# A two-block transformer kernel: who loads the constants, how piece 0 is rounded, and who closes the last norm

## The reference

```python
h = rmsnorm(x, attn_norm[layer])
x = x + even_mixer(h, even_w_in[e], ...)          # layer 0: h @ w_in comes first
...
f = (jax.nn.gelu(gate, approximate=True) * val) @ w_down[l]
h = h + rms_norm(f, ln_ffn_post[l])               # the end: x * rsqrt(mean(x*x) + eps) * gain, plus h
return h
```

## Time and profile before

| | us |
|---|---|
| median of 3 runs (lowest, highest) | 1922.12 (1921.83, 1923.32) |
| the profiled execution | 1921.35 |
| its span, first to last instruction | 1919.6 |
| TensorE busy | 1888.2 (98%) |
| VectorE busy | 997.7 (52%) |
| ScalarE busy | 740.3 (39%) |
| GpSimd busy | 179.4 (9%) |

### The profile page before, as it was taken

How to read it: one execution, slowest core, us unless ns; L and a number is a source line. 1 busy time by engine, 2 the same in 40 slices (tenths; PEclk the granted TensorE clock), 3 DMA queues, 4 the chain that set the end, 5 groups by cost and what they waited for, 6 DMA issues and landing times.

```text
span 1919.6 us, 26779 instructions
## 1 busy us (share of the span) xinstructions
PE 1888.2 (98%) x10729; PEld 1527.4 (80%) x10729; DVE 997.7 (52%) x1418; ACT 740.3 (39%) x1111; POOL 179.4 (9%) x215
## 2 busy tenths in 40 slices
PE   9999999999999999999999999999999999999998
PEld 7875788888888777788888888777879778888887
DVE  5456443434335686553343434759563576656523
ACT  4247432222234575542222323554342454333322
POOL 2001210000001100010000000303551100000001
PEclk9999999999999999999999999999999999999999
DMA  6310132232322202123223232321120223232321
GB/s 209 97 45 1 50 108 90 87 109 87 110 87 80 72 23 67 45 91 107 90 87 109 88 110 88 101 88 44 24 68 25 88 79 108 87 108 88 109 88 66
DMA packets 137795, 158.74 MB, mean 83 GB/s; under 512 B 15976, under 2 KB 125552, under 8 KB 137712
## 3 DMA queue, kind: packets, MB, share of 16 engines
q1 hardware_dynamic: 136272, 155.01, 24.9%
q0 software_dynamic: 1440, 2.58, 0.4%
HBM read 153.89 MB, written 3.68 MB: 82 GB/s over the span
## 4 chain that ended last, share of the span: by engine, by line
PE 91%; DVE 6%; ACT 2%; issue 1%; POOL 0%; ACTq 0%; DVEq 0%
PE bank L2894 35%; PE bank L2927 17%; PE bank L2426 14%; PE bank L2451 3%; PE bank L2981 2%; PE bank L2570 2%; PE bank L2945 2%; PE bank L2840 1%; PE bank L2873 1%; PE bank L2598 1%; PE bank L2689 1%; PE bank L2585 1%; PE bank L2512 1%; PE bank L2542 1%; DVE XL L1590 1%
## 5 line engine op out<-in xcount | busy, mean ns | idle before, releaser
L2894 PE MATMUL bank<-XH,w_hi 128*128 128x512 f32 x992 | 386.8, 390 | 0.7 <-DVE arena L1890 0.7
L2894 PE MATMUL bank<-XH,w_lo 128*128 128x512 f32 x992 | 385.9, 389 | 0.0
L2894 PE MATMUL bank<-XL,w_hi 128*128 128x512 f32 x992 | 385.9, 389 | 0.0
L2894 PEld LDWEIGHTS bank<-XH,w_hi 128*128 128x128 f32 x992 | 186.2, 188 | 40.0 <-DVE arena L1890 0.9
L2894 PEld LDWEIGHTS bank<-XL,w_hi 128*128 128x128 f32 x992 | 186.2, 188 | 38.9 <-issue 0.5
L2894 PEld LDWEIGHTS bank<-XH,w_lo 128*128 128x128 f32 x992 | 186.2, 188 | 38.8
L2426 PE MATMUL bank<-XH,w_hi 128*128 128x512 f32 x448 | 178.9, 399 | 2.6 <-DVE w_lo L1583 2.4
L2426 PE MATMUL bank<-XL,w_hi 128*128 128x512 f32 x448 | 175.2, 391 | 0.0
L2426 PE MATMUL bank<-XH,w_lo 128*128 128x512 f32 x448 | 175.0, 391 | 0.0
L1583 DVE TENSOR_TENSOR w_lo<-w_raw,w_hi 128x2048 fp32r<-128x2048 f32 (+5 forms) x67 | 116.4, 1757 | 94.0 <-ACT w_hi L1037 93.6
L1937 DVE TENSOR_TENSOR w_lo<-w_raw,w_hi 128x2048 fp32r<-128x2048 f32 x24 | 55.0, 2292 | 173.2 <-ACT w_hi L1348 173.2
(11 more groups left out here) (459 smaller groups left out, 3333.6 us busy)
## 6 DMA issues: line engine op xcount, KB each, us to landing
w_raw<-in_ffn_w_gate SPq DMA_DIRECT2D x22, 1024.0 KB, 5.1
w_raw<-in_ffn_w_up SPq DMA_DIRECT2D x22, 1024.0 KB, 5.1
w_raw<-in_ffn_w_down SPq DMA_DIRECT2D x22, 1024.0 KB, 4.8
w_raw<-in_w_up SPq DMA_DIRECT2D x22, 1024.0 KB, 4.9
w_raw<-in_w_in SPq DMA_DIRECT2D x13, 1024.0 KB, 5.1
w_raw<-in_w_down SPq DMA_DIRECT2D x11, 1024.0 KB, 4.9
w_raw<-in_even_w_in SPq DMA_DIRECT2D x8, 1024.0 KB, 5.0
w_raw<-in_even_w_out SPq DMA_DIRECT2D x4, 1024.0 KB, 5.0
```

The source lines that it names most:

```text
L2894: m = pe.matmul(bank[b][:, :], w[:, k, P * c:P * (c + 1)], x[:, k, :], start=(k == 0 and j == 0), stop=(k == KT - 1 and j == 2))
```

## The change

- The loads of the constants and of the vectors are issued by ScalarE's queue, as its first two instructions, and no more by SyncE.
- The warm-up of TensorE has four matmuls, not five.
- `XH` of piece 0 is made from bank 4 directly. ScalarE waits for the vectors and the transposed piece; VectorE's copy of piece 0 from the bank to `X` now waits for this rounding (`norm_hi`), and `low` of piece 0 waits for the copy's own increment.
- At the end VectorE multiplies the second half of each row block by the gain row as soon as the sums are there (`gained`), and, when the reciprocal root has come, scales that product and adds the residual in one operation (`closed`). The first halves of blocks 0 to 2 go as before (scaling by VectorE, add by GpSimd). In the last block both halves go the new way, and the first half is multiplied before the second half's square is there. SyncE's waits follow.

```diff
--- before.py
+++ after.py
@@ -768,9 +768,6 @@
 
         @block.sync
         def _(sp):
-            sp.dma_start(con[:, 0:2 * P], d["const_cols"][:, 0:2 * P]).then_inc(setup_loaded, 16)
-            sp.dma_start(vrow[:, :, :], d["vec_rows"].rearrange("(a p) n -> p a n", p=P)).then_inc(setup_loaded, 16)
-
             def load(slot, src):
                 kt, n = src.shape[1], src.shape[2]
                 dst = w_raw[:, slot, 0:kt * n].rearrange("p (t n) -> p t n", n=n)
@@ -857,10 +854,10 @@
             for t in range(ST):
                 rows = slice(P * t, P * (t + 1))
                 for n in range(2):
-                    if t == ST - 1 and n == 1:
-                        sp.wait_ge(normed_out, KT + 1)
+                    if t == ST - 1 or n == 1:
+                        sp.wait_ge(normed_out, KT + t + 1 + (t == ST - 1 and n == 1))
                     else:
-                        sp.wait_ge(out_added, 2 * t + n + 1)
+                        sp.wait_ge(out_added, t + 1)
                     cols = slice(512 * n, 512 * (n + 1))
                     sp.dma_start(out[0][rows, cols], fin[:, t, cols]).then_inc(stored, 16)
             sp.wait_ge(stored, 16 * 2 * ST)
@@ -924,11 +921,10 @@
                     gains = d["vec_rows"][at:at + KT, :].rearrange("a p -> (a p)").unsqueeze(0)
                     pool.wait_ge(normed_out, KT)
                     pool.dma_start(gain_row, gains.broadcast_to([P, D])).then_inc(side_loaded, 16)
-                    for t in range(ST):
-                        for n in range(2 if t < ST - 1 else 1):
-                            o = feature_blocks(fin[:, t, 512 * n:512 * (n + 1)])
-                            pool.wait_ge(scaled_out, KT + 2 * t + n + 1)
-                            pool.tensor_tensor(o, o, token_major(n, t), ALU.add).then_inc(out_added, 1)
+                    for t in range(ST - 1):
+                        o = feature_blocks(fin[:, t, 0:512])
+                        pool.wait_ge(scaled_out, KT + 2 * t + 2)
+                        pool.tensor_tensor(o, o, token_major(0, t), ALU.add).then_inc(out_added, 1)
                 if s == "mla":
                     sum_squares("mla")
                     sum_squares("q")
@@ -1017,6 +1013,9 @@
         def _(act):
             links = [0]
 
+            act.dma_start(con[:, 0:2 * P], d["const_cols"][:, 0:2 * P]).then_inc(setup_loaded, 16)
+            act.dma_start(vrow[:, :, :], d["vec_rows"].rearrange("(a p) n -> p a n", p=P)).then_inc(setup_loaded, 16)
+
             def link(ins):
                 links[0] += 1
                 ins.then_inc(act_link, 1)
@@ -1240,7 +1239,9 @@
                     high(name, k)
 
             def even():
-                high("even", 0)
+                act.wait_ge(turned_out, 1)
+                act.wait_ge(turned, 2)
+                act.activation(XH[:, 0, :], bank[4][:, :], ACT.Copy, scale=gain_of("even", 0)).then_inc(norm_hi, 1)
                 act.wait_ge(w_first, 16)
                 act.activation(w_hi[:, 0, 0:1024], w_raw[:, 0, 0:1024], ACT.Copy).then_inc(w_hi_ready, 1)
                 for k in range(1, 4):
@@ -1730,8 +1731,11 @@
             def even():
                 for f in range(KT):
                     dve.wait_ge(turned, f + 2)
+                    if f == 0:
+                        dve.wait_ge(norm_hi, split_base["even"] + 1)
                     dve.tensor_copy(X[:, f, :], bank[4 + f % 4][:, :]).then_inc(turned_out, 1)
                     if f == 0:
+                        dve.wait_ge(turned_out, 2)
                         low("even", 0)
                     if f == 1:
                         dve.wait_ge(w_hi_ready, 1)
@@ -1992,19 +1996,34 @@
 
             def last_norm():
 
+                def gained(t, n):
+                    cols = slice(512 * n, 512 * (n + 1))
+                    dve.tensor_tensor(fin[:, t, cols], bank[2 * t + n][:, :], gain_row[:, cols], ALU.mult)\
+                       .then_inc(scaled_out, 1)
+
+                def closed(t, n):
+                    o = feature_blocks(fin[:, t, 512 * n:512 * (n + 1)])
+                    dve.scalar_tensor_tensor(o, o, frstd[:, t:t + 1], token_major(n, t), ALU.mult, ALU.add)\
+                       .then_inc(normed_out, 1)
+
+                last = ST - 1
                 dve.wait_ge(side_loaded, 64)
                 for t in range(ST):
+                    if t == last:
+                        dve.wait_ge(sq_ready, n_sq + 2 * t + 1)
+                        gained(t, 0)
                     dve.wait_ge(sq_ready, n_sq + 2 * t + 2)
                     dve.scalar_tensor_tensor(fmean[:, t:t + 1], fsq[:, 2 * t:2 * t + 1], EPS, fsq[:, 2 * t + 1:2 * t + 2],
                                              ALU.add, ALU.add).then_inc(out_mean, 1)
+                    gained(t, 1)
                     dve.wait_ge(rstd_ready, len(NORMS) + t + 1)
-                    for n in range(2):
-                        cols = slice(512 * n, 512 * (n + 1))
-                        dve.scalar_tensor_tensor(fin[:, t, cols], bank[2 * t + n][:, :], frstd[:, t:t + 1],
-                                                 gain_row[:, cols], ALU.mult, ALU.mult).then_inc(scaled_out, 1)
-                o = feature_blocks(fin[:, ST - 1, 512:D])
-                dve.wait_ge(scaled_out, KT + 2 * ST)
-                dve.tensor_tensor(o, o, token_major(1, ST - 1), ALU.add).then_inc(normed_out, 1)
+                    if t < last:
+                        dve.scalar_tensor_tensor(fin[:, t, 0:512], bank[2 * t][:, :], frstd[:, t:t + 1],
+                                                 gain_row[:, 0:512], ALU.mult, ALU.mult).then_inc(scaled_out, 1)
+                    dve.wait_ge(scaled_out, KT + 2 * t + 1 + (t == last))
+                    if t == last:
+                        closed(t, 0)
+                    closed(t, 1)
 
             def taps(i, c, half, t):
 
@@ -3320,7 +3339,7 @@
                     rows(k, stop=(k == 3))
 
             pe.wait_ge(setup_ready, 1)
-            for j in range(5):
+            for j in range(4):
                 pe.matmul(bank[2][:, 0:2 * P], sq_acc[:, 0:P], sq_acc[:, 0:2 * P], start=True, stop=True)
             pe.wait_ge(setup_loaded, 32)
             for j in range(3):
```

## The result

| | before | changed |
|---|---|---|
| median, 22 executions each | 1922.02 | 1925.24 |
| lowest, highest | 1919.79, 1923.47 | 1922.65, 1927.76 |
| the profiled execution | 1921.35 | 1922.65 |
| its span | 1919.6 | 1920.8 |

The changed kernel is slower: ratio 1.0018, 95% interval 1.0012 to 1.0024, about 3.2 us. The forecast was 1921.6, in a range from 1920.0 to 1923.4: the measured median lies above it. The loss is just under the 0.2% that the prediction named as measurable; with 22 executions of each the interval excludes no change.

The account below looks back on a forecast made before the run. TensorE, busy 98% of the span, was taken as the bound, leaving the first 13 and last 6 us. Opening -0.7 and end +0.2 took 1922.12 to 1921.6 us, range 1920.0 to 1923.4.

Parts of the forecast that it names:

- Opening, the queue: Opening: constants issued by ScalarE let SyncE's loads be issued 0.9 us earlier; piece 4's landing taken as 0.7 us earlier.
- The DMA gate: Opening: piece 4's landing, which holds TensorE until about 12.9 us; said to move -0.7, bounds 0 and -0.9.
- the first rival: Opening: landings don't move, piece 4 stays at 12.3, the opening gives 0, total 1922.3; chance 0.2.
- rival 5: Opening: constants on ScalarE's queue land later; landing at 5.7 would cost 0.5 of the 0.7, total 1922.1; chance 0.05.
- Opening, the chain: Opening: shorter warm-up and direct rounding move VectorE's series about -0.7 us; first product near 9.0 instead of 9.85.
- rival 4: Opening: shorter warm-up leaves TensorE at its lower clock longer; opening +0.6, first product at 10.2, total 1922.9; chance 0.08.
- End: Last row blocks: the new split, with GpSimd's additions holding VectorE's means, costs +0.2 us, bounds -1.1 and +1.1.
- Rivals 2 and 3: End: GpSimd's additions come ahead of closings, +1.1, 1922.5; or the exclusion doesn't hold, -1.1, 1920.3; chance 0.12 each.
- the bound without exclusion: End: VectorE and GpSimd don't hold each other up, last closing at 1915.97, so -1.1 us.
- the rule was read from other rows: End: a VectorE operation with two SBUF inputs and a GpSimd addition exclude each other; whoever comes second waits.

Follow-up runs that it names:

- warm_only: Kernel before with four warm-up matmuls instead of five; median 1922.33, ratio 1.0004 (0.9995 to 1.0013).
- rest_only: Changed kernel with the two loads of constants and vectors back on SyncE's queue; median 1921.83, ratio 0.9998 to the kernel before.
- end_vector: Kernel before with the new end made on VectorE alone, no additions by GpSimd; median 1920.53, ratio 0.9999 (0.9990 to 1.0008).
- end_only: Kernel before with only the new closing of the last norm; median 1921.53, ratio 0.9999 (0.9990 to 1.0008).

## Why the prediction was wrong

- **Opening, the queue: the step that failed.** "The DMA gate, bounds 0 and -0.9; I take -0.7." In the trace it was +0.1: piece 4 landed at 12.4, where I had 11.6 and where it was 12.3 before. The slow stretch of the earlier trace rows was read as a hole that earlier work fills; it moved along. This step accounts for 0.7 of the 3.6 us between forecast and result. This is the first rival, which had 0.2, and the rule of the Trainium skill in "DMA: Bandwidth & Descriptors", "Issuing engines are not separate DMA queues", that only issue time is saved: the trace agrees for the weights and piece 4, issued 0.9 and 1.4 us earlier and landed 0.1 later. Piece 0 did land 2.0 us earlier, at the vectors' cost, which landed 1.6 later.
- **The missing bound: the step that cost most.** Worse than the size was the sign. I bounded the edit at 0 on the side of loss, and priced constants that come late (rival 5) at 0.5 of the gain with a chance of 0.05. Moved alone the constants cost 3.2 and 3.1 us. The rows on record showed enough to be wary: 320 KB that had a start of 0.9 us over SyncE's other loads were to lose it.
- **Opening, the chain: right in order, short in size.** First product at 9.40 (said 9.0), XL of piece 1 over at 12.56 (said 12.2). The vectors' transposes began at 5.41 by their landing, not by the warm-up, which cost 0.2 us. The first product then stood behind the transposes of piece 1, which waited 0.87 us for that piece and began at 8.79, and XL of piece 0 was over only at 9.26; the prediction had no term for the landing of piece 1. One matmul of warm-up less and the direct rounding alone gave nothing that can be measured, as a gate on DMA at 12.3 to 12.4 says they must.
- **Warm-up and clock (rival 4).** Not in the changed kernel's trace, where the fillers took 1.46, and warm_only's interval (ratio 1.0004) holds no change. But rest_only's trace has what the rival describes, fillers of 2.72 and a first product at 10.67 (said 10.2), so it can happen; how often it does in the executions without a trace is not known.
- **End: right.** Said +0.2, measured +0.12; means said to be held by up to 1.2, 0.61 to 0.97 measured; additions said 1.75, 1.70 to 1.73 measured. Who comes first is as said: the closing, then the addition, which then holds the next mean. Rivals 2 and 3 fall by the same rows. For the bound without exclusion, -1.1, the nearest measurement is end_vector's -0.75. That the sizes came out so close is earned: the rule was read from other rows and gave the length of each mean within 0.2 us.
- **Outside the terms.** The clock's low stretches come at different places, and the profiled execution was taken for the usual one: here it is the shortest of 22.

**What stays open.** The mechanism inside the timed executions. It needs three conditions together, and each was taken away alone: both groups of constants on the second queue, SyncE's loads behind piece 0 issued at once beside them, and TensorE taking them up one by one. One guess is that the constants, or a piece, land still later there than the 5.3 of the traces, and that TensorE stays at its lower rate in the opening for longer, as in rest_only's (whose median has no loss, though). No trace shows it, so it is argued and not shown; and about 2 of the 3 us are there at an equal recorded clock, so a low clock at a later stage is at most a third of it. The cause of the 3 us stays open; what is shown is the edit that brings it and three conditions without which it goes.

## What to carry to other kernels

Here a second issuing queue brought the weights and piece 4 no earlier, though they were issued 0.9 to 1.4 us earlier; it brought piece 0 forward by 2.0 us and the vectors, wanted first, back by 1.6. Give the loads that are wanted first their head start, and bound such an edit on the side of loss too. Before work is moved between VectorE and GpSimd, look at which operations on VectorE have two inputs in SBUF: one of a single column took 0.61 to 0.97 us instead of 0.16 beside GpSimd additions.

## What the runs showed of the hardware that I had not expected

- Issuing SyncE's first loads 0.9 us earlier moved the slow stretch of the transfers (100 GB/s between 3 and 4 us before; 342 there in the changed kernel, with 200 and 169 between 5 and 7), so it is no gap that waits to be filled.
- One kernel's profiled executions (1920.48, 1920.74, 1920.89, 1921.15) lay 3 to 4 us under the medians of its two sets of eleven (1924.26, 1924.25), while for end_only the profiled one was 1921.70 beside a median of 1921.53. A trace need not hold the effect that the timing has.
- Two traces of one and the same opening (the kernel before and end_only) put the products of piece 1 at 12.95 and 13.72, and such a difference is handed on unchanged to 180 us (0.78 and 0.75 at the same instructions of ScalarE). One trace of each kernel can't tell 0.1 us in the opening from nothing.
